# A bidirectional hybrid backbone on one core: the delta-rule layers' decay exponents in three buffers, their steps at other positions of the slot, and identities copied in earlier

## What is computed

```python
p = h @ w_in
qkv = silu(centred_dwconv(p[..., :GDN_CONV_DIM], conv_w)); z = p[..., GDN_CONV_DIM:...]
q = l2norm(q) * 128 ** -0.5; k = l2norm(k)          # each q/k head serves two v heads
beta = sigmoid(b); g = -exp(a_log) * softplus(a + dt_bias)
# gated_delta_chunked, per head and direction, chunk after chunk:
gc = cumsum(g)
decay = exp(where(incl, gc[:, None] - gc[None, :], -inf))
a_mat = where(strict, (k * beta) @ k.T * decay, 0)
t_mat = a_mat + eye
u, w = triangular_solve(t_mat, [v * beta, k * beta * exp(gc)])
qk = q @ k.T * decay
v_new = u - w @ s; o = (q * exp(gc)) @ s + qk @ v_new
s = s * exp(gc[-1]) + (k * exp(gc[-1] - gc)).T @ v_new
# finish: rmsnorm(o_forward + o_backward, g_norm) * silu(z) @ w_out
```

## Time and profile before

| | |
|---|---|
| median of 3 runs | 3356.7 us (3348.37 to 3357.59) |
| the profiled execution | 3356.15 us, of which the span from first to last instruction is 3354.4 |
| TensorE matmul, weight load | 3133.7 us (93%), 2045.9 us (61%) |
| VectorE, ScalarE, Pool | 1884.8 us (56%), 1461.9 us (44%), 825.8 us (25%) |
| mean granted TensorE clock | 0.975 |
| layer 0's slots, layer 3's slots | about 66.7 and 57.6 us each |

### The profile page before, as it was taken

The page is one execution under the profiler, slowest core; times in us unless marked ns, Lnnn a source line. Parts: engine busy times, 40 slices in busy tenths (PEclk is TensorE's granted clock), DMA queues, the critical chain, the costliest instruction groups (busy, mean ns, idle before and its releaser), DMA issues. The chain is left out here.

```text
span 3354.4 us, 56002 instructions
## 1 busy us (share of the span) xinstructions
PE 3133.7 (93%) x22057; PEld 2045.9 (61%) x22057; DVE 1884.8 (56%) x3609; ACT 1461.9 (44%) x2963; POOL 825.8 (25%) x588
## 2 busy tenths in 40 slices
PE   5879999999999999999999999897999999999998
PEld 2347776777767764455545565444777676667663
DVE  1147676767676762234542344345777777777742
ACT  3125445544544451145532444333555554555521
POOL 0023433433343320001101011002433434343400
PEclk9789999999999999999999999898999999999999
DMA  9811211221121116112302111202111222121135
GB/s 376 307 56 48 60 54 43 63 56 55 44 68 50 48 46 218 67 46 62 128 16 57 32 45 40 80 2 70 57 58 58 62 59 62 52 73 52 52 109 193
DMA packets 224098, 261.96 MB, mean 78 GB/s; under 512 B 19418, under 2 KB 158948, under 8 KB 223716
## 3 DMA queue, kind: packets, MB, share of 16 engines
q1 hardware_dynamic: 223844, 258.46, 23.9%
HBM read 239.15 MB, written 19.27 MB: 77 GB/s over the span
## 5 line engine op out<-in xcount | busy, mean ns | idle before, releaser
L895 PE MATMUL ps<-hT,W 128*128 128x512 f32 (+1 forms) x2656 | 999.1, 506 | 5.5 <-ACT arena L1128 3.5
L895 PEld LDWEIGHTS ps<-hT,W 128*128 128x128 f32 x2656 | 471.3, 193 | 203.7 <-issue 172.1
L1314 DVE CAST_PREDICATED arena<-mask,ps 128x384 bf16<-128x384 uint32 x448 | 252.3, 563 | 184.3 <-PE ps L964 176.6
L1145 ACT CAST arena<-ps 128x384 bf16<-128x384 f32 x384 | 167.8, 482 | 364.8 <-PE ps L951 363.6
L2349 PE MATMUL ps<-arena 128*128 128x512 f32 x712 | 311.1, 595 | 2.8 <-SPq L192 2.8
L1316 DVE CAST_PREDICATED arena<-mask,ps 128x384 bf16<-128x384 uint32 x448 | 250.2, 558 | 0.0
L2349 PEld LDWEIGHTS ps<-arena 128*128 128x128 f32 x712 | 134.6, 191 | 167.6 <-issue 162.6
L1984 PE MATMUL ps<-hT,W 128*128 128x512 f32 (+1 forms) x608 | 218.2, 493 | 0.8 <-DMA W<-in_att_w_in 0.6
L1433 POOL TENSOR_TENSOR arena<-arena,cst 128x768 f32<-128x768 f32 x64 | 117.0, 1850 | 390.2 <-DVE arena L1283 390.2
L1474 POOL TENSOR_TENSOR arena<-arena 128x768 f32<-128x768 f32 (+1 forms) x32 | 49.2, 1537 | 613.4 <-DVE arena L1377 613.4
L1295 DVE SCALAR_TENSOR_TENSOR arena<-arena,vec 128x770 f32<-128x770 f32 (+1 forms) x192 | 195.4, 1017 | 6.8
(11 more groups left out here) (280 smaller groups left out, 6288.8 us busy)
## 6 DMA issues: line engine op xcount, KB each, us to landing
arena<-in_ada_w SPq DMA_DIRECT2D x24, 2048.0 KB, 19.5
W<-in_gdn_w_in SPq DMA_DIRECT2D x95, 512.0 KB, 4.0
arena<-decay_sums SPq DMA_DIRECT2D x64, 384.0 KB, 3.9
W<-decay_rows SPq DMA_DIRECT2D x64, 384.0 KB, 5.0
arena<-in_gdn_w_out SPq DMA_DIRECT2D x32, 512.0 KB, 10.5
W<-in_gdn_w_out SPq DMA_DIRECT2D x30, 512.0 KB, 3.4
arena<-gated SPq DMA_DIRECT2D x32, 384.0 KB, 7.7
gated<-arena SPq DMA_DIRECT2D x24, 384.0 KB, 2.4
```

The lines of the kernel that those rows point to most:

```text
L895: mm = pe.matmul(ps[:, b, 0:t1 - t0], w[:, i, :], env.hT[:, i, t0:t1], start=(i == 0), stop=(i == KD - 1))
L1145: act.copy(half_cols(Xb[d], s, d), ps[:, 2 * d, 0:384].rearrange("p (c b s) -> p c b s", c=NT, s=s)).then_inc(*inxe.up(m, lv, d))
L1314: dve.copy_predicated(half_cols(Mb[d], s, d), wide(env.m4[:, d, lv]), src_m).then_inc(*inm.up(m, lv, d, "m"))
```

## The change

The decay exponents get a third buffer, and SyncE loads and Pool caps a unit one slot sooner (unit n + 3 in slot n). VectorE's column sums (`exponents`) move from position 11, unit n + 2, to position 15, unit n + 3. ScalarE's exponentials for unit n + 2 move from position 13 to 3. VectorE's `matrix` moves for odd units from the slot's end to position 12; for even units it stays. The copies of the second and third correction product go into `NATb` and `NLOb` instead of `Mb` and `MTb`. So Pool can write a unit's identities in the slot before: into `Mb` after the residual products, into `MTb` after VectorE's L1325, both behind the query scaling in its list. Pool's bf16 copy into `NLOb` now waits for the last correction product of the unit before. Slot -2 does the first unit's column sums at position 11 and its exponentials at 13, and Pool does its caps and identities first of all.

```diff
-G_AT = 11
-EXP_AT = 13
+G_AT = 15
+EXP_AT = 3
+NAT_AT = 12
...
-                    ("gexp", (2, T), 2), ("table", (4 * NT * 2, 16))])
+                    ("gexp", (2, T), 3), ("table", (4 * NT * 2, 16))])
...
-                sp.dma_start(v.gexp[m % 2][:, d], a["sums"][d, m].partition_broadcast(P)).then_inc(*gl.up(m, d))
+                sp.dma_start(v.gexp[m % 3][:, d], a["sums"][d, m].partition_broadcast(P)).then_inc(*gl.up(m, d))
...
-            if n > -2 and n + 2 in U:
-                sp.wait_ge(gcap.sem, gcap.at(n + 1, 1))
+            if n + 3 in U:
+                sp.wait_ge(gcap.sem, gcap.at(n + 2, 1))
                 sp.wait_ge(qkd.sem, qkd.at(n, 1))
-                load_g(n + 2)
+                load_g(n + 3)
...
-                        mm = pe.matmul(unit(d, c), Xb[d][:, c], Mb[d][:, c], start=False, stop=True, skip_group_check=True)
+                        mm = pe.matmul(unit(d, c), Xb[d][:, c], NATb[d][:, c], start=False, stop=True, skip_group_check=True)
...
-                        mm = pe.matmul(unit(d, c), Xb[d][:, c], MTb[d][:, c], start=True, stop=True)
+                        mm = pe.matmul(unit(d, c), Xb[d][:, c], v.NLOb[d][:, c], start=True, stop=True)
...
-                    act.copy(halves(Mb[d]), both_banks(d)).then_inc(*rev.up(m, 1, d))
+                    act.copy(halves(NATb[d]), both_banks(d)).then_inc(*rev.up(m, 1, d))
...
-                    act.copy(halves(MTb[d]), both_banks(d)).then_inc(*rev.up(m, 2, d))
+                    act.copy(halves(v.NLOb[d]), both_banks(d)).then_inc(*rev.up(m, 2, d))
...
-                if p == EXP_AT and n + 2 in U:
+                if p == (EXP_AT if n > -2 else 13) and n + 2 in U:
                     decay(n + 2)
...
-                if p == G_AT and n + 2 in U:
-                    exponents(n + 2)
+                if p == 11 and n == -2:
+                    exponents(0)
+                if p == G_AT and n + 3 in U:
+                    exponents(n + 3)
+                if p == NAT_AT and n % 2 and n + 2 in U:
+                    matrix(n + 2)
...
-            if n + 2 in U:
+            if n % 2 == 0 and n + 2 in U:
                 matrix(n + 2)
...
+        def ones_on_diagonal(m):
+
+            for d in BOTH:
+                pool.wait_ge(rf.sem, rf.at(m - 1, "r0", d))
+                pool.tensor_copy(Mb[d], idb).then_inc(*minit.up(m, d, "m"))
+            for d in BOTH:
+                pool.wait_ge(m1.sem, m1.at(m - 1, d))
+                pool.tensor_copy(MTb[d], idb).then_inc(*minit.up(m, d, "t"))
+
+        capped(0)
+        ones_on_diagonal(0)
         for n in SLOTS:
             m = n + 1
             if m in U:
                 for d in BOTH:
-                    pool.wait_ge(rf.sem, rf.at(m - 1, "t2", d))
-                    pool.tensor_copy(Mb[d], idb).then_inc(*minit.up(m, d, "m"))
-                for d in BOTH:
-                    pool.wait_ge(rf.sem, rf.at(m - 1, "t3", d))
-                    pool.tensor_copy(MTb[d], idb).then_inc(*minit.up(m, d, "t"))
-                for d in BOTH:
...
+                    pool.wait_ge(rf.sem, rf.at(m - 1, "t3", d))
                     pool.tensor_copy(v.NLOb[d], NAT[d]).then_inc(*nlo.up(m, d, "mid"))
...
-            if n + 2 in U:
-                capped(n + 2)
+            if n + 3 in U:
+                capped(n + 3)
...
+            if m in U and m + 1 in U:
+                ones_on_diagonal(m + 1)
```

More of the change, by code:

```diff
@@ L1160, in decay @@
                 act.wait_ge(garg.sem, garg.at(m, d))
-                act.activation(v.gexp[m % 2][:, d], v.gexp[m % 2][:, d], ACT.Exp).then_inc(*gexp.up(m, d))
+                act.activation(v.gexp[m % 3][:, d], v.gexp[m % 3][:, d], ACT.Exp).then_inc(*gexp.up(m, d))
         def values(m, s):
@@ L1334, in exponents @@
                 dve.wait_ge(gcap.sem, gcap.at(m, d))
-                g = v.gexp[m % 2][:, d].rearrange("p (c n) -> p c n", c=NT)
+                g = v.gexp[m % 3][:, d].rearrange("p (c n) -> p c n", c=NT)
                 dve.tensor_tensor(g, g, tab[:, COL, :, d, m:m + 1].broadcast_to([P, NT, P]), ALU.add).then_inc(*garg.up(m, d))
@@ L1343, in matrix @@
                 dve.wait_ge(nlo.sem, nlo.at(m - 1, d, "low"))
-                dve.tensor_tensor(flat(NAT[d]), flat(v.KK), v.gexp[m % 2][:, d], ALU.mult).then_inc(*natd.up(m, d))
+                dve.tensor_tensor(flat(NAT[d]), flat(v.KK), v.gexp[m % 3][:, d], ALU.mult).then_inc(*natd.up(m, d))
         def score(m):
@@ L1350, in score @@
                 dve.wait_ge(ro.sem, ro.at(m - 1, NT - 1, d))
-                dve.tensor_tensor(flat(QKD[d])[:, LO:T], v.gexp[m % 2][:, d, LO:T], flat(v.QK)[:, LO:T], ALU.mult).then_inc(*qkd.up(m, d))
+                dve.tensor_tensor(flat(QKD[d])[:, LO:T], v.gexp[m % 3][:, d, LO:T], flat(v.QK)[:, LO:T], ALU.mult).then_inc(*qkd.up(m, d))
         def scan(m, p):
```

## The result

The changed kernel takes 3299.1 us (median of four runs, 3295.2 to 3300.4) where the kernel before takes 3356.1 beside it: ratio 0.983, 95% interval 0.982 to 0.985, so 57 us faster. The forecast was 22.7 us, 3333.5, in a range that began at 3317, 18 us above what was measured. The direction was right, the size was not. The profiled execution took 3300.44 us, its span is 3298.7, and its mean granted clock is 0.975 as before.

What follows compares the result with a forecast made beforehand. TensorE, busy 65.8 of 66.6 us in a slot, was taken as the bound, only its idle time winnable. Terms of -43.2 and +20.5 gave net -22.7 from 3356.15, so 3333.5 us; own range 3321 to 3346, 8-in-10 range 3317 to 3354.

Steps and rivals of the forecast that it cites:

- collision at position 15: Odd slots: column sums meet Pool's query scaling, delaying TensorE's L982; +9.8 us in layer 0, +3.5 in layer 3.
- Exponentials: Layer 0's even slots: at position 3, logarithm starts earlier, gap 0.7 instead of 2.31 us, six times: -9.6 us.
- Odd matrix: Even-slot starts: without the matrix, scores and level 0 come earlier; -9.5 us in layer 0, -7.0 in layer 3.
- Slot 14: Layer 0, slot 14: ScalarE's bf16 copies no longer delay the logarithm; gap 3.46 becomes about 1.5, -2.0 us.
- Identities: Odd-slot starts: even units' matrix runs without Pool's identity copies; -9.1 us in layer 3, 0 in layer 0.
- Matrix at position 12: Odd slots: matrix meets an idle Pool; 0.2 us reach TensorE in layer 3, seven times: +1.3 us.
- Start of the layers: Slot -2, layers 0 and 3: Pool's caps of unit 1 delay the first square; +5.9 us, bounds 2 and 9.
- Clock: Layer 0: five low-clock stretches behind gaps fall to one or two; -6.0 us, bounds 0 and -8.5.
- no collision: Position 15: column sums and Pool's scaling don't collide, 13.3 us are not paid; 3320 us, chance 0.13.
- third rival: Odd slots, position 15: VectorE's sums lose every turn to Pool, pair takes 7.2 us; slower, 3365 us, chance 0.08.

Runs made afterwards that it cites:

- the kernel with both undone: Changed kernel with identities written at the slot's start again and the odd units' matrix at the slot's end again; 3345.0 us, ratio 0.996.

## Why the forecast was right in direction and wrong in size

Forecast -22.7, traces -55.7. The step that failed most is the price of the collision at position 15: 13.3 us booked, none paid. Behind it come what was booked at nothing, layer 0's odd starts with L940 and L1025 at its even ones (8.1) and the wait at the sums' old place (4.2), and the starts of layer 3's slots, too small by 6.3. By its own steps, each difference taken from the starts of the same matmuls:

- **Exponentials, -9.6.** Right: -8.8, six times 1.46, from 2.31 to 0.85.
- **Odd matrix, -9.5 in layer 0, -7.0 in layer 3.** The gains at the even starts are there (-11.1 and -9.1), but they are not the matrix's alone. What failed here is that I costed each edit against the profile of before, with the other absent. I took the matrix at its undisturbed 1.83 us from the earlier trace rows; at the even starts it took 2.95 under Pool's copies (shown above in the kernel with both undone), and that alone made the two edits one question. In the sum the error cancels, since both edits are in the change; in the attribution it does not: alone in the kernel before, the identities make 40.5 of the 66.7 us won in the slots.
- **Slot 14, -2.0.** Right, -2.5.
- **Identities: -9.1 in layer 3, 0 in layer 0.** Layer 3's odd starts gave 13.3, 1.9 each: 1.50 of the 1.61 us of the gaps went, and 0.4 more. Layer 0's odd starts gave 5.2, and L940 with L1025 at its even starts 2.9 more. I had booked nothing there because Pool's subtraction would slide under the scores. It does, but the pair of scores then takes 3.27 us, not 3.89: that longer pair had also met identity copies. The upper bound of 5.6 was the better value.
- **Collision at position 15, +9.8 and +3.5.** This term failed most: 0. It took the duration of the pair from a row where Pool had started first. Here VectorE starts first, by 0.16 us. With the order turned, the chip charges 11.1 us in the slots, near my 13.3; so the way to L982 and its margin were read rightly, and the order of the two starts was not asked for. The forecast called both "released by L1418"; but VectorE's next instruction needs no signal from it, and began 0.08 us before L1423's recorded end, and Pool 0.08 us after it. The Trainium skill, "SBUF — State Buffer", section "SBUF: two separate sides", says that where a VectorE instruction has two SBUF inputs and a Pool one reads SBUF, whichever starts first holds the shared ports for its whole instruction while the other blocks. With that rule the traces agree, 3.44 and 4.96 us for the same pair; the prediction cited only that there is contention.
- **Sums leaving position 11, not in the sum.** L1010 (L1009 before) lost its wait, six times 0.69, -4.2; with the sums back at position 11 3.7 of it came back. The earlier trace rows show the 4.94 us pair, but I asked only what it costs at its new place, not who waited behind it at the old one.
- **Matrix at position 12, +1.3.** Nothing to be seen.
- **Start of the layers, +5.9.** Mechanism right, 12.3 in size, 10.7 of it at the first norm products, which wait for the square. I had taken the list in front of the square as starting no later than before and the caps at their undisturbed 3.59; beside the convolution the first took 4.57. The upper bound was 9.
- **Clock, -6.0.** All five stretches went, 1.4 to 1.7 us each, -7.9, near the outer bound of 8.5.
- **Tails, not in the sum.** Where a gap goes altogether, TensorE gains more than the idle time that the profile shows: 1.85 for 1.59 at L1032, 0.69 for 0.28 at L1009, 1.9 for 1.50 and 1.5 for 1.17 at layer 3's odd and even starts. Where part of the gap stays, it gains just the difference: 1.46 at L901, 0.37 at L1032 of the odd starts, 2.48 in slot 14. The idle time is counted from the end of the matmul before, and without a wait the next one begins before that end: at an odd start of layer 3 in the changed kernel L942 begins at 2392.61 and takes 0.33, and L940 begins at 2392.78. In the slots of both layers the idle time shown fell by 44.6 us and the clock gave 7.9, while 66.7 us were won; some 14 us are such tails. They are contained in the sizes above; a forecast by idle time misses them.

The differences add up: collision 13.3, layer 0's odd starts with L940 and L1025 8.1, L1010 4.2, sizes of the gaps in layer 0 1.3, clock 1.9, layer 3's starts 6.3 and its matrix term 1.3, 3.0 unassigned (1.3 in layer 3's slots, 0.4 in layer 0's, 1.3 outside them), less 6.4 for the starts of the layers: the 33.0 by which the trace missed the sum. Of the rivals "no collision" came nearest, at 3320, but with one term changed it was only two fifths of the way. Too narrow was the range as well: the bounds of the single terms (0 for the collision, -5.6, -8.5, 0 for the matrix) were taken as if only one of them could come out at its end. All of them together, with 2 for the start of the layers, would have been 26.6 us lower, 3307, and still above what was measured, because the old place of the sums and the tails had no term.

Two figures beside the sum don't come out either. The gaps that the prediction lists in its first part add up to 51 us, not 45. And in its third rival the pair of 7.2 us would stall TensorE by 3.8 us in layer 3, not 2.8, worked as for layer 0 (free at 2464.80, 1.5 more for the residual, against 2469.66); that rival is then 7 us slower. The forecast rests on neither.

## What to carry to other kernels

Where two edits relieve the same wait, work out what each is worth with the other in place; most of the waits at the even starts went with either, and came back only without both. Where VectorE and Pool meet on operands in SBUF, ask which of them starts first and which of them can afford to wait, and place the instruction so that the engine on the path comes first: here 0.32 us of delay cost 11 us in the slots. And of a step that moves, price the place that it leaves as carefully as the place that it goes to.

## What the hardware showed beyond that

- One and the same pair of VectorE instructions, 1.82 us alone, took 3.44 us when it started 0.16 us before Pool's pair, and 4.94 to 4.96 when Pool was ahead; Pool's pair, 3.58 alone, took 4.96 and 4.30. Pool's bf16 copies of the identities hold VectorE up too: pairs of 1.82 us alone took 2.95 and 3.07 beside them, and the convolution of three instructions took 6.43 us beside caps and copies and 3.13 beside an idle Pool.
- A gap of 2.3 us ahead of the norm products was followed by 3.4 us at the 1.2 GHz level six times in six in the kernel with the exponentials back, three times in six in the kernel before (the earlier trace rows is such a stretch) and twice in six in the kernel before with early identities; a gap of 0.85 never in the changed kernel. What decides between two, three and six the runs don't show.
- Layers 1 and 2, where no kernel has an edit, took 1024.7 to 1025.1 us in six of the fourteen traces, before and after among them, 2.0 less in one, and 7.7 to 9.1 less in seven. The time that they run at 0.50 clock goes with it in all fourteen: 27 to 31 us in the six, 24 in the one, 7 to 10 in the seven. Half of the difference, 10 us, is about the time that is missing. Why the same instructions fall into one case or the other stays open. Differences of 8 us between two of these medians are therefore not yet differences between the edits.
